# Selection of a group's second tile dealt out from 9 batches ahead of the group's gather to 28 into it, in place of 2 to 56

## What is computed

```python
def block(xt):
    q = (xt @ w_pq).reshape(PEER_BLOCK, PEER_HEADS, 2, half)
    s1 = jnp.einsum('thc,nc->thn', q[:, :, 0], sub_keys1)
    s2 = jnp.einsum('thc,nc->thn', q[:, :, 1], sub_keys2)
    v1, i1 = lax.top_k(s1, PEER_TOPK)
    v2, i2 = lax.top_k(s2, PEER_TOPK)
    cand = (v1[..., :, None] + v2[..., None, :]).reshape(PEER_BLOCK, PEER_HEADS, PEER_TOPK * PEER_TOPK)
    sc, ci = lax.top_k(cand, PEER_TOPK)
    e1 = jnp.take_along_axis(i1, ci // PEER_TOPK, axis=-1)
    e2 = jnp.take_along_axis(i2, ci % PEER_TOPK, axis=-1)
    idx = e1 * PEER_NKEYS + e2
    g = jax.nn.softmax(sc.astype(F32), axis=-1).astype(xt.dtype)
    act = jax.nn.gelu(jnp.einsum('td,thkd->thk', xt, peer_u[idx]), approximate=False)
    return jnp.einsum('thk,thkd->td', g * act, peer_v[idx])
```

## Time and profile before

| | |
|---|---|
| median of 3 runs | 4257.27 us |
| lowest and highest | 4254.24 and 4258.38 us |
| the profiled execution | 4264.31 us |
| its span | 4262.5 us |
| instructions | 48896 |
| VectorE busy | 2708.3 us (64%) |
| PE busy | 3112.3 us (73%) |
| ScalarE busy | 1513.0 us (35%) |
| gather, software DMA queue | 1107.36 MB, 65.1% of the sixteen engines' time |
| all DMA | 1499.19 MB, mean 352 GB/s |

### The profile page before, as it was taken

The page is one execution under the profiler, slowest core; times in us unless marked ns, Lnnn a source line. Parts: engine busy times, 40 slices in busy tenths (PEclk is TensorE's granted clock), DMA queues, the critical chain, the costliest instruction groups (busy, mean ns, idle before and its releaser), DMA issues. The chain is left out here.

```text
span 4262.5 us, 48896 instructions
## 1 busy us (share of the span) xinstructions
PE 3112.3 (73%) x15864; PEld 1989.7 (47%) x15864; DVE 2708.3 (64%) x7617; ACT 1513.0 (35%) x3085; POOL 1253.3 (29%) x1068
## 2 busy tenths in 40 slices
PE   6787688898788769788887679788776676633333
PEld 4676565676555327555554347454442364400000
DVE  1326357437667884578568874596678845776775
ACT  3533366312255651113555540133456611010010
POOL 0000112112233332333233332333333323354453
PEclk8798888899888779899878789888787788855555
DMA  7485767788989989999889899999999999999997
GB/s 263 142 323 188 285 237 260 270 312 336 361 342 373 359 313 398 394 417 404 352 353 361 335 368 385 414 399 400 382 387 383 373 414 413 396 415 415 414 404 329
DMA packets 269366, 1499.19 MB, mean 352 GB/s; under 512 B 44969, under 2 KB 81673, under 8 KB 97465
## 3 DMA queue, kind: packets, MB, share of 16 engines
q0 software_dynamic: 152064, 1107.36, 65.1%
q1 hardware_dynamic: 117048, 388.70, 24.2%
HBM read 1463.49 MB, written 31.36 MB: 351 GB/s over the span
## 5 line engine op out<-in xcount | busy, mean ns | idle before, releaser
L1711 POOL DMA_INDIRECT rt_ring<-in_peer_uv,rt_few_idx x1056 | 1250.0, 1184 | 2979.8 <-PE rt_acc L886 2344.6
L1657 DVE SCALAR_TENSOR_TENSOR rt_ring<-rt_ring,rt_h 128x1024 f32<-128x1024 f32 x1056 | 1267.6, 1220 | 541.2 <-DMA rt_ring<-in_peer_uv,rt_few_idx 536.6
L886 PE MATMUL rt_acc<-rt_ring,rt_diag 128*32 128x512 f32 x4224 | 762.4, 797 | 602.3 <-DVE rt_diag L1668 600.4
L635 PE MATMUL pair<-dense,w 128*128 128x256 f32 (+2 forms) x3056 | 599.4, 355 | 25.8 <-DMA w<-in_weights 24.2
L635 PEld LDWEIGHTS pair<-dense,w 128*128 128x128 f32 x3056 | 518.2, 198 | 140.7 <-issue 62.9
L624 PE MATMUL pair<-w,dense 128*128 128x256 f32 (+1 forms) x2352 | 557.8, 395 | 7.0 <-DVE dense L1313 2.8
L1212 ACT ACTIVATE rt_act_dot<-rt_dot 128x2 f32<-128x2 f32 x528 | 106.0, 202 | 1271.7 <-DVE rt_ring L1657 1262.5
L886 PEld LDWEIGHTS rt_acc<-rt_ring,rt_diag 128*32 128x32 f32 x4224 | 100.9, 122 | 930.1 <-DVE rt_diag L1668 789.3
L624 PEld LDWEIGHTS pair<-w,dense 128*128 128x128 f32 (+1 forms) x2352 | 437.5, 189 | 159.1 <-issue 73.7
L1668 DVE TENSOR_SCALAR rt_diag<-cst,rt_act_dot,rt_few_prob 128x32 f32<-128x32 f32 x1056 | 266.2, 297 | 82.6 <-ACT rt_act_dot L1212 64.1
L635 PE MATMUL bank<-dense,w 128*128 128x256 f32 (+2 forms) x1424 | 276.0, 350 | 1.4 <-DMA w<-in_weights 0.9
(11 more groups left out here) (241 smaller groups left out, 3314.5 us busy)
## 6 DMA issues: line engine op xcount, KB each, us to landing
w<-in_weights SPq DMA_DIRECT2D x284, 1024.0 KB
rt_ring<-in_peer_uv,rt_few_idx POOLq DMA_INDIRECT x1056
dense<-scratch_mod SPq DMA_DIRECT2D x18, 512.0 KB, 11.0
dense<-in_x_prompt SPq DMA_DIRECT2D x16, 512.0 KB, 10.3
rt_h<-scratch_h SPq DMA_DIRECT2D x33, 128.0 KB
rt_x<-scratch_x SPq DMA_DIRECT2D x132, 32.0 KB
out_k_prompt<-dense SPq DMA_DIRECT2D x32, 128.0 KB
out_v_prompt<-dense SPq DMA_DIRECT2D x32, 128.0 KB
```

Of the source, the lines that this page charges most:

```text
L635: mm = nc.tensor.matmul(bank[b][:, 0:n], wt[:, k * CH + j * P:k * CH + (j + 1) * P], src[:, k, 0:n], start=(k == 0), stop=(k == KC - 1))
L886: mm = nc.tensor.matmul(acc[u % 2][a * T:(a + 1) * T, :], diag[b % 2][:, i, :], slot[:, D + c * BANK:D + (c + 1) * BANK], start=(q == 0), ...
L1657: dt = nc.vector.scalar_tensor_tensor(up, up, 1.0, h2[u % 2][:], ALU.mult, ALU.mult, accum_out=dot[:, b % 2, i:i + 1])
L1711: nc.gpsimd.indirect_dma_start(ring[n % RING][:], None, d["peer_uv"], bass.IndirectOffsetOnAxis(ap=few_idx[u % 2][:, c:c + 1], axis=0)).th ...
```

## The change

One line of `sequence()` changes, the row of `sides` for a group's second tile. `start` is the first batch of the group's gather (64, 192, 320 or 448) and `n` the number of batches of the first tile, 64.

```diff
         for ti, t in enumerate(tiles[:-1]):
             n = NB * (COPIES if t < NT else 1)
-            sides.append((tiles[ti + 1], start + 2, start + n - 8, select(tiles[ti + 1], 0)))
+            sides.append((tiles[ti + 1], start - 9, start + 28, select(tiles[ti + 1], 0)))
             start += n
```

## The result

The changed kernel takes 4229.8 us (median of 4 runs, 4226.3 to 4232.8) against 4257.8 us (4 runs, 4254.2 to 4262.4) for the kernel before in the same comparison. The ratio is 0.9936, 95% interval 0.9921 to 0.9951, so 28 us less; the forecast was 4238, 20 us less. In a second comparison the same kernel came to 4228.5 us, ratio 0.9918 (0.9896 to 0.9939). The mean of the two ratios is 0.9927.

A forecast was written before the change was run, and what follows sets the result against it. Attention was taken as held up by VectorE or its waits, query projection as nearly full on VectorE and DMA. Groups -9, -8, -0.5 and end -2 gave -19.5 us: 4238 from the median 4257.3, range 4218 to 4264.

The forecast's parts named there:

- Attention: Attention of groups (3,4), (5,6) and (7,8): selection that leaves it gains 21, 23 and 9.5 us.
- light steps: Selection steps 0 to 39, searches of about 1.15 us; 0.4 to 0.5 of their time shows in attention.
- heavy ones: Selection steps 41 to 46, one 2048-wide pass of 2.28 us each; 0.9 of their time shows in attention.
- The pairs of the earlier trace: Two-batch attention units of group (5,6): about 12.2 us with light steps, mean 15.77 with two heavy steps.
- Query projection: Query projections of groups (5,6) and (7,8): arriving heavy steps cost 7.5 and 4 us, VectorE and DMA both full.
- Batches 87 to 93: First group, end of linear attention, 1324.4 to 1372.4: arriving heavy steps cost 6 us.
- Value projection and linear attention: Stages ahead of query projection: 25.8, 26.7 and 27.2 us of selection arrive; a quarter shows, 6, 7.5 and 5 us.
- The end: Group (7,8) in the gather's own time: denser selection costs nothing, -2 us, bounds -3 and +3.
- the queues: Second tile's index and probability loads reach SyncE three batches earlier, ending its stand: nothing, 3 us gain as bound.
- (a): Rival: attention bound by exponential, score, maximum; 36 us gained against 36 paid, about 4257, no change; chance 0.24.
- (b): Rival: everything leaving attention shows, 77 us less 36 paid ahead, about 4216; chance 0.14.
- (c): Rival: steps in linear attention delay Gelu, weighted sum and gather; 66 us at eight tenths, about 4275; chance 0.14.

The follow-up runs named there:

- e2: Against the kernel before, only selection steps 0 to 39 dealt out early, steps 40 to 47 left in attention: 4231.6 us, ratio 0.9936.
- q1: Changed kernel plus 18 VectorE reductions of 2.28 us in single attention batches without the maxima that wait for scores: 4237.4 us, ratio 0.9939.
- q2: Changed kernel plus 18 VectorE reductions of 2.28 us in single attention batches with the maxima that wait for scores: 4280.2 us, ratio 1.0046.
- p1: Changed kernel plus 18 VectorE reductions of 2.28 us, in six attention batches in a row per group, three groups: 4249.9 us, ratio 0.9979.
- p2: Changed kernel plus 18 VectorE reductions of 2.28 us in the query projections, six per group: 4267.7 us, ratio 1.0024.
- u1: Changed kernel with the second tile posted at start + 56, as before, in place of start + 53: 4233.4 us, ratio 0.9926.
- p4: Changed kernel plus 18 VectorE reductions of 2.28 us in batches where VectorE waits for gathers, six per group: 4231.2 us, ratio 0.9941.
- p3: Changed kernel plus 18 VectorE reductions of 2.28 us in the last batches of linear attention, six per group: 4262.0 us, ratio 1.0011.
- e3: Changed kernel with the second tiles' steps dealt out in 30 batches in place of 38, ending at start + 20: 4228.3 us, ratio 0.9921.
- e1: Kernel before with the change in the first group alone (tile 2), the others keeping the old rule: 4244.4 us, ratio 0.9961.

## Why the forecast was right, and which terms were off

**Attention: right in sum, wrong in its parts, and the sum owes something to luck.** The forecast took 21 + 23 + 9.5 = 53.5 us out of it; the two traces show 56.8 and 51.4. But it gave the light steps 0.4 to 0.5 and the heavy ones 0.9; e2 shows light 0.72 and 0.59 in the first two groups and heavy 0.7 and 0.8. A share too low for the one and too high for the other made up for each other. The reason given, that a step ahead of the wait for the scores only shortens that wait, is what q1 shows (0.1 to 0.2, though nearly half in group (5,6)), and the step in the other batch costs more than the full price in two groups (q2). The pairs of the earlier trace rows were read as heavy steps being on the path by kind. In q1 and q2 the price goes by place, and the heavy steps stood in both places, one in each batch of a unit. In the third group e2 shows 0.1 us for the light steps, at 391 GB/s; that the DMA decides there, as the forecast said, fits this, and the lower prices of q1, p1 and q2 in that group.

**Query projection: right.** Forecast 7.5 and 4, measured 6.8 and 2.6, for 10.1 and 7.5 us more of VectorE's busy time. A part fell on time in which VectorE had been idle, 5.1 and 5.6 us before and 1.7 and 0.6 after. p2's price of 0.9 to 1.0 is that of work that comes on top. Batches 87 to 93 gave 4.5 and 4.7 for 6.

**Value projection and linear attention: too dear, the mis-sized term.** Forecast 6 + 7.5 + 5 = 18.5; measured 5.8 and 11.0 in sum, with 2.0 and 1.2 in place of 7.5 in group (5,6). All that arrives ahead, with the query projections, was charged 36 us and cost 19 and 24. Two things were mis-sized. What arrives was counted with 1.15 us a light step; VectorE's busy time grew by 20.0, 20.8 and 21.2 us in place of 25.8, 26.7 and 27.2. And a quarter was taken for the whole stage, though before, selection ran from `start + 2` on already, so that 13 of the 22 steps that arrive in group (5,6) land in batches 183 to 193. Seven traces have the changed kernel's order there with no pad in it (the two, u1, p1, p2, q1 and q2), and they agree. Batches 183 to 193 are 4.3 to 6.3 us longer, and batches 194 to 213, which hold nine more steps, are 2.9 to 4.1 us shorter. So the steps cost a third to a half where they land, and most of it is won back behind them. The wait for the gather shrank from 32.5 to 14.0 us in the whole stage (the earlier trace rows against the waits above), and most of that in batches 194 to 213, here in the kernel before (2101.4 to 2240.6) and in the changed kernel (2086.8 to 2223.2):

```profile
DVE rt_ring L1657 <- DMA rt_ring<-in_peer_uv,rt_few_idx: 20.4, 12, 3.8
...
DVE rt_ring L1657 <- DMA rt_ring<-in_peer_uv,rt_few_idx: 5.8, 6, 1.5
```

p4 fits in two groups of three; in (5,6) its pads cost 4.5 of 13.7 us, in batches 198 to 203, where the changed kernel has only 4.6 us of this wait left. Why the gather is less late once the steps come earlier isn't shown.

**The end and the queues.** -2.5 and -1.0 us for -2, but that can't be told from nothing: the other seven kernels with the same end (u1, p1 to p4, q1, q2) show -1.2 to +0.8. What repeats in all nine traces is small: the batches that lost the heavy steps (496 to 504) are 1.2 to 2.2 us shorter, those that got them (471 to 479) 0.4 to 1.0 longer. Nothing for the queues is right as far as u1 and e2 can tell.

**The rivals.** (a) is out: it had the heavy steps about right (0.75), but the light ones at a quarter, and it needed all 36 us ahead; the pairs that held the heavy steps take 12 us. (b), all 77 us shown, is out: 51 to 57 did. (c) had a mechanism that the pads bear out: VectorE work added in the second head pair's linear attention costs 0.5 to 0.9 (p3), around its deciding point of 0.65. It didn't decide because the 66 us that it was multiplied with were too many (62 us of busy time arrive in the three groups, the first included), because few of them land on such batches, and because in (5,6) the time is won back, against what (c) says. e3, which does put the heavy ones there, loses what the query projection gives back.

**The signs that were to be looked for.** Pairs at 12 to 13 us throughout: 12 from batch 238 on, but 12.6 to 14.3 in batches 226 to 233. Attention at 340 to 370 GB/s: 354 and 359, the third 399, for which the range was too low. Query projection longer by 7: 6.8. The end at 5.06 to 5.1 us a batch: 5.2 with the heavy steps, 5.14 in the same batches before. SyncE's stand gone: yes. VectorE's wait for PE L795 grown to 35 us: no, 27.9. By q1, taking steps from ahead of that wait should lengthen it; why it didn't when the selection left isn't shown.

The gain was 28 us (35 in the second comparison) for a forecast of 20. The 12 to 17 us overcharged ahead of attention cover that difference; what remains is inside the spread of the unchanged stages. So the forecast was right by its mechanism, that attention loses more than the stages ahead gain, and its total came near by sizes that were off in both directions.

## What to carry to other kernels

Where one engine runs two chains in order, price added or moved work by the wait that stands next behind it, not by the engine's busy share: in these runs work ahead of a wait cost 0.1 to 0.2 of its length, and the same work behind it more than its own length. Take the length of work from the engine's busy time over a stretch, not from a sum of instruction durations, since short instructions overlap. Before moving work out of a full stage, split what arrives by batch: the price differs between batches of one stage, and time lost in one batch may be won back in the next ones. A few dummy instructions of known length, shifted by one batch, give that price in one run each.

## What the runs showed of the hardware that was not expected

The granted clock in attention was higher after the change: 0.72 to 0.82 in group (3,4), 0.73 to 0.80 in (5,6), 0.78 both times in (7,8) (0.82, 0.78 and 0.80 in the second trace), and with it the same matmuls of (3,4) went from 99.9 to 89.5 us. It was not forecast, and of the 20 us gained in that stage no run tells how much is the clock's. A part of such differences has nothing to do with the order of the work. In e1, which has the order of before in attention (5,6), the matmuls there take 125.5 us at 0.77, against 133.3 at 0.73 in the kernel before:

```profile
2274.70:2475.20 200.50, 125.49 (x626) 62.13 (x626) 171.79 (x417) 112.17 (x182) 64.30 (x56) 0.77 0.87 340
...
2289.90:2494.70 204.80, 133.27 (x626) 66.14 (x626) 171.66 (x416) 111.93 (x182) 68.59 (x56) 0.73 0.86 329
```

The same holds for the whole kernel. PE's busy time was 3112 us before and 3087 and 3089 in the changed kernel's two traces, with the same 15864 instructions; but u1, which differs from the changed kernel only in the place of a few loads, has 3098 us. So some 10 of the 25 us may be one execution against another.

POOL's issues of the gather are mostly of two lengths in the profile, whose times for POOL are rough. After batch 430 of the kernel before, those that run beside one of the two-input dot products (L1657) for 0.3 us or more have a median of 1.81 us (104 of them), and the 77 that run beside neither a dot product nor a 2048-wide pass take 0.94. So the means of the earlier trace rows, 1279 and 1400 ns, are mixtures of the two, and their difference says little of the heavy passes: the four beside the one-input sum L1633 have a median of 0.94 us too.
